# Expert stage of a routed MoE: row writes of further groups without a wait behind their issue, and the activation transpose inside the next expert's first product

## Chip, cores and metric

The kernel runs on one core of one Trainium2 chip. The metric is the device time of one execution in microseconds (us), as the median of several runs. An engine's names are as in the profile: PE is TensorE's matmul side and PEld its weight loads, DVE is VectorE, ACT is ScalarE, POOL is GpSimd, SP is SyncE, which here issues all plain DMAs.

## What is computed

One step of a decoder trunk with one layer, for 512 prompt tokens and 8 sample tokens of width 1024, all in float32. A mixer sub-layer (three parallel head groups behind one input projection, one output projection) comes first; the change doesn't touch it. The second sub-layer is the one that matters: a mixture of 32 experts, each a SwiGLU MLP with an inner width of 256.

```python
g_idx = argmax(h @ w_group)                                # one of 4 groups of experts
top_p, top_i = top_k(softmax(h @ w_router[g_idx]), 2)      # two of its 8 experts
combine = ...                                              # the weight of each expert for each token
gate = einsum('btd,edf->btef', h, w_gate)                  # w_gate, w_up: (32, 1024, 256)
up = einsum('btd,edf->btef', h, w_up)
act = silu(gate) * up * combine[..., None]
out = x + einsum('btef,efd->btd', act, w_down)             # w_down: (32, 256, 1024)
```

The kernel computes each expert only for the tokens routed to it.

## The kernel before

The expert stage stands at the end of the program, from about 546 to 850 us of the profiled execution. Ahead of it, VectorE ranks the tokens of each expert, and GpSimd scatters their numbers with ten indirect DMAs into `slot_table` (`tab` in the code). An expert has 64 slots (`CAP`); tokens past the 64th go to *further groups* of 64 slots. How many further groups an expert has is only known at run time: each engine loads the number from `more` and branches (`more_groups`), so each of PE, ACT, DVE and POOL runs its own `body` under the same conditions.

Experts are taken four to a round (`ROUND = 4`, u = 0 to 3), eight rounds, of which the first and the last are written out and the six between are a hardware loop. There are four weight slots, one for each u. SP loads an expert's `w_gate`, `w_up` and `w_down` (1 MB each) into slot u with three DMAs once VectorE has counted `expert_done` for the expert that used the slot before (`load_expert`); VectorE counts it after the expert's last copy, that of its further groups included. All these loads are in SP's queue in the order of the experts.

For each expert e, PE does the following:

- `up`: the first product, gate and up side by side, 16 steps in the code (8 chunks of the 1024 inner rows, for each half of the columns), 32 matmuls in the trace. It waits for the expert's weights and for `xT`, the gathered and transposed tokens of a pair of experts.
- a transpose of `gact`, the activations, into PSUM bank 2 (line 1952). Before it, ACT has taken the tanh of the gate (`tanh_gate`), and DVE has made `gact` of it in two instructions (`swiglu`, lines 1531 and 1533).
- `down`: the second product with `aT`, the transposed activations that ACT has copied out of PSUM (`act_T`), into bank 4 or 5. DVE copies the result to `ysb`, and POOL writes the rows to `expert_rows` (`yd` in the code) with an indirect DMA.

The products are staggered: within a round PE does `up` of experts 0 and 1, then the transpose and `down` of expert 0, `up` of expert 2, transpose and `down` of expert 1, `up` of expert 3, and so on; u = 3 has no `up` behind it. After the `up` of u = 0 and u = 2 PE also transposes the tokens of the next pair (`xg`, line 1949), which ACT copies to `xT` (`xT_out`). The rows `xg` are gathered by POOL with an indirect DMA.

A further group of expert e stands behind its `down`. POOL has gathered its rows to `xo[u % 2]`: for an expert's first group this happens two experts ahead, at the end of POOL's work for expert e - 2 (`first_further`, which calls `gather_more`: index to `otok` at line 1076, gather at line 1081). PE transposes the rows (lines 1962 and 1964), computes `up` into bank 3, transposes the activations (line 1969) and computes `down`, again into bank 3, with ACT and DVE between the steps, and DVE copies the result to `yo`. POOL writes `yo` out with one indirect DMA (line 1064, named `expert_rows<-yo,osid`). Three waits close this:

```python
# POOL, behind the write
pool.wait_ge(m_out, done * 16 + 16)
pool.sem_inc(m_saved, 1)
# DVE, ahead of the copy to yo
vec.wait_ge(m_saved, done + 1)
# PE, behind its last product of the group (bank 3 is free when yo is copied)
pe.wait_ge(m_vec, done * 3 + 3)
```

`done` counts the further groups that came before. On the inputs here there are four further groups, one each for the experts 17, 19, 23 and 24 (rounds 4, 4, 5 and 6).

Of the kernel before, what the change touches and what calls it, by code (L numbers as in the profile page):

```python
# [13 lines left out]
P = 128  # L26
D = 1024
KT = D // P
# [82 lines left out]
def build(nc, A, R):  # L111

    with ExitStack() as ctx:
# [246 lines left out]
        def pair(name):  # L360
# [33 lines left out]
        m_otok, m_osid, m_pe, m_act, m_vec, m_out, m_saved = (  # L394
            sem("more_" + n) for n in ("otok", "osid", "pe", "act", "vec", "out", "saved"))
# [61 lines left out]
        def _(sp):  # L457
# [94 lines left out]
            sp.wait_ge(tab_written, 2 * NT * 16)  # L552
# [31 lines left out]
        def _(act):  # L584
# [279 lines left out]
            def act_round(it, first, last):  # L864
                for u in range(ROUND):
                    e = ROUND * it + u
                    if u == 1 or (u == 3 and not last):
                        xT_out(2 * it + (u + 1) // 2, (u + 1) // 2 % 2)
                    if u < 3:
                        if u == 0:  # L870
                            tanh_gate(e, 0)
                        tanh_gate(e + 1, (u + 1) % 2)
                    act_T(e, u % 2)

                    def body(g, done, needed):
                        act.wait_ge(m_pe, done * 4 + 1)
                        copy(xTo[:, :, :].rearrange("p a b -> p (a b)"), ps[:, 3, :], ACT.Copy).then_inc(m_act, 1)
                        act.wait_ge(m_pe, done * 4 + 2)
                        copy(oth[:, :], ps[:, 3, 0:P], ACT.Tanh, scale=0.5).then_inc(m_act, 1)
                        act.wait_ge(m_pe, done * 4 + 3)  # L880
                        copy(oaT[:, :], ps[:, 3, 0:P], ACT.Copy).then_inc(m_act, 1)

                    more_groups(act, e, body)
# [26 lines left out]
        def _(pool):  # L910
# [97 lines left out]
            for i in range(NT):  # L1008
                pool.wait_ge(routed, 3 if i < SPLIT else 6)
                for n in range(2):  # L1010
                    nc.gpsimd.indirect_dma_start(out=tab, out_offset=bass.IndirectOffsetOnAxis(ap=where[:, n, i:i + 1], axis=0),  # L1011
                                                 in_=pid[:, n, i:i + 1], in_offset=None, bounds_check=MAXROWS * NE - 1,
                                                 oob_is_err=False).then_inc(tab_written, 16)
# [4 lines left out]
            pool.sem_inc(m_saved, 1)  # L1018
# [18 lines left out]
            def pool_round(it, first, last):  # L1037
                for u in range(ROUND):
# [16 lines left out]
                    def body(g, done, needed):  # L1055
                        nc.gpsimd.tensor_tensor(osid[:, :], osids[:, bass.ds(g * NE + column, 1)], zero[:, :], ALU.add).then_inc(
# [5 lines left out]
                        pool.wait_ge(m_vec, done * 3 + 3)  # L1062
# [4 lines left out]
                        pool.wait_ge(m_out, done * 16 + 16)  # L1067
                        pool.sem_inc(m_saved, 1)
# [27 lines left out]
            for u in range(ROUND):  # L1096
                pool.wait_ge(y_out[u], 16 * ROUNDS)
            pool.sem_inc(moe_done, 1)

        @block.vector  # L1100
        def _(vec):
# [423 lines left out]
            count_groups(vec, "vec")  # L1525
            vec.wait_ge(routed, 7)
# [9 lines left out]
            def vec_round(it, first, last):  # L1536
                for u in range(ROUND):
# [10 lines left out]
                    def body(g, done, needed):  # L1548
                        vec.wait_ge(m_act, done * 3 + 2)
                        stt(out=oact[:, :], in0=oth[:, :], scalar=1.0, in1=ps[:, 3, 0:P], op0=ALU.add, op1=ALU.mult).then_inc(m_vec, 1)  # L1550
                        vec.wait_ge(m_vec, done * 3 + 1)
                        stt(out=oact[:, :], in0=oact[:, :], scalar=0.5, in1=ps[:, 3, P:2 * P], op0=ALU.mult, op1=ALU.mult).then_inc(m_vec, 1)
                        vec.wait_ge(m_pe, done * 4 + 4)
                        vec.wait_ge(m_saved, done + 1)
                        nc.vector.tensor_copy(yo[:, :], ps[:, 3, :]).then_inc(m_vec, 1)
# [30 lines left out]
        def _(pe):  # L1586
# [329 lines left out]
            def halves(bank, left, right, steps, width):  # L1916
                for c in range(steps):
# [4 lines left out]
            def up(u, bank, left):  # L1922

                return halves(bank, left, lambda c, g: gu[u][:, :, c, g * P:(g + 1) * P], KT, 2 * P)

            def down(u, bank, a):
                return halves(bank, lambda c: a[:, c * CAP:(c + 1) * CAP], lambda c, g: wd[u][:, c, g * 512:(g + 1) * 512], 2, 512)

            def pe_up(it, u):
                e = ROUND * it + u  # L1930
                s = u // 2
                pe.wait_ge(weights_in[u], tiles_in[u] + 3 * 16 * (it + 1))
                pe.wait_ge(xT_ready, 2 * it + s + 1)
                up(u, u % 2, lambda c: xT[s][:, c, u % 2 * CAP:(u % 2 + 1) * CAP]).then_inc(up_done, 1)

            def pe_round(it, first, last):
                for u in range(ROUND):
                    e = ROUND * it + u
                    if u == 0:
                        pe_up(it, 0)  # L1940
                    if u < 3:
                        pe_up(it, u + 1)
# [8 lines left out]
                    pe.wait_ge(act_ready, e + 1)  # L1951
                    turn(ps[:, 2, 0:P], gact[u % 2][:, :], ident).then_inc(act_turned, 1)
# [3 lines left out]
                    def body(g, done, needed):  # L1956
                        pe.wait_ge(m_rows[u % 2], pe.snap(slot_groups[u % 2]) * 16 + 16)
                        pe.reg_add(slot_groups[u % 2], slot_groups[u % 2], 1)
                        for c in range(KT):
# [8 lines left out]
                        pe.wait_ge(m_vec, done * 3 + 2)  # L1968
# [3 lines left out]
                        pe.wait_ge(m_vec, done * 3 + 3)  # L1972
# [31 lines left out]
```

## Time and profile before

| | |
|---|---|
| time, median of 3 runs | 879.26 us (878.67 to 883.45) |
| profiled execution: span from its first to its last instruction | 876.5 us |
| what lies around the span, against the median | 2.8 us |
| PE, PEld busy | 680.9 us (78%), 493.8 us (56%) |
| DVE, ACT, POOL busy | 378.6, 201.0, 239.2 us |
| the mean DMA rate over the span, and in the expert stage at its fullest | 167 and 412 GB/s |
| the mean granted clock of PE | 0.895 of full |

The page of the profile gives no other time for the profiled execution than its span. Busy time is an average over stages with different limits: in the expert stage the loads of 96 MB of expert weights, PE's products and the short chains between the engines take turns in setting the pace, and a window or a chain of waits has to be read for each stretch.

### The profile page before, as it was taken

What the parts mean: (1) busy time and instruction counts of PE and PEld (TensorE: products, weight loads), DVE (VectorE), ACT (ScalarE), POOL (GpSimd) and SP (SyncE); (2) the same over time, 40 slices, a digit from 0 to 9 for tenths busy, and PEclk for the clock granted to TensorE, in tenths of its full rate; (3) what the DMA queues carried; (4) which work ended last, traced back from release to release, by engine and by line L of the source; (5) the groups of instructions that cost most, each with busy time, mean ns of one, the idle gap of its engine ahead of it and who ended that gap; (6) DMA issues with size and microseconds to landing.
All of it is one profiled execution on the core that took longest, in us unless ns stands there. A gap on an engine that the chain in (4) does not pass through costs nothing.

```text
span 876.5 us, 12140 instructions
## 1 busy us (share of the span) xinstructions
PE 680.9 (78%) x4468; PEld 493.8 (56%) x4469; DVE 378.6 (43%) x570; ACT 201.0 (23%) x401; POOL 239.2 (27%) x268
## 2 busy tenths in 40 slices
PE   2699978789889999978898840978889766978840
PEld 2699977679778889854344430544444433444410
DVE  3605999997347666546212453112112110111128
ACT  5113325634222341241001110101101110101103
POOL 1527479975230010110000024122122221321210
PEclk9989989889989999995889965899989997999985
DMA  9013322112071000035111541299999975895926
GB/s 278 26 49 98 97 73 71 51 49 54 6 247 65 1 1 1 1 118 198 32 48 49 191 168 28 69 413 408 410 414 405 410 310 213 313 386 222 404 75 246
DMA packets 73209, 146.70 MB, mean 167 GB/s; under 512 B 14568, under 2 KB 50604, under 8 KB 64831
## 3 DMA queue, kind: packets, MB, share of 16 engines
q1 hardware_dynamic: 67327, 137.38, 42.7%
q0 software_dynamic: 5824, 8.54, 2.8%
q8 instruction: 37, 0.61, 0.3%
q14 instruction: 21, 0.17, 0.1%
HBM read 139.65 MB, written 16.60 MB: 178 GB/s over the span
## 4 chain that ended last, share of the span: by engine, by line
PE 51%; DVE 25%; DMA 13%; issue 4%; ACT 4%; POOL 1%; SPq 1%; POOLq 0%; DVEq 0%; ACTq 0%
PE ps L1919 17%; DMA wd<-w_down 8%; PE ps L1709 8%; PE ps L1859 7%; PE ps L1636 7%; DVE yT L1179 6%; DVE acc L1189 4%; DMA xo<-h_rows,otok 1%; DVE XX L1355 1%; PE ps L1880 1%; DVE cv L1197 1%; DVE x L1568 1%; PE ps L1949 1%; PE ps L1619 1%; PE ps L1842 1%
## 5 line engine op out<-in xcount | busy, mean ns | idle before, releaser
L1919 PE MATMUL ps<-gu,xT 128*64 128x256 f32 x1024 | 128.3, 409 | 30.2 <-DMA wd<-w_down 15.0
L1636 PE MATMUL ps<-hhi,whi 128*128 128x256 f32 (+1 forms) x416 | 125.1, 301 | 18.7 <-POOL wlo L927 8.3
L1919 PEld LDWEIGHTS ps<-gu,xT 128*64 128x64 f32 x1024 | 80.6, 148 | 85.5 <-issue 35.4
L1636 PE MATMUL ps<-hhi,wlo 128*128 128x256 f32 (+1 forms) x416 | 122.9, 295 | 0.0
L1636 PE MATMUL ps<-hlo,whi 128*128 128x256 f32 (+1 forms) x416 | 122.7, 295 | 0.0
L1636 PEld LDWEIGHTS ps<-hhi,whi 128*128 128x128 f32 x416 | 84.4, 203 | 24.7 <-POOL wlo L927 15.9
L927 POOL TENSOR_TENSOR wlo<-wraw,whi 128x1024 fp32r<-128x1024 f32 x26 | 77.1, 2971 | 66.5 <-ACT whi L609 66.4
L1636 PEld LDWEIGHTS ps<-hhi,wlo 128*128 128x128 f32 x416 | 84.5, 203 | 0.0
L1636 PEld LDWEIGHTS ps<-hlo,whi 128*128 128x128 f32 x416 | 84.2, 202 | 0.0
L1531 DVE SCALAR_TENSOR_TENSOR gact<-gth,ps 128x128 f32<-128x128 f32 x32 | 9.2, 288 | 148.6 <-ACT gth L891 148.6
L1919 PE MATMUL ps<-wd,aT 128*64 128x512 f32 x256 | 62.0, 605 | 11.7 <-ACT aT L895 11.7
L1051 POOL DMA_INDIRECT expert_rows<-ysb,scur x32 | 32.4, 1014 | 141.0 <-DVE ysb L1546 137.4
L1859 PE MATMUL ps<-wout,yT 128*128 128x512 f32 x128 | 65.6, 671 | 0.0
L1179 DVE SCALAR_TENSOR_TENSOR yT<-ub,parab,yT 128x512 f32<-128x512 f32 x60 | 63.0, 1115 | 0.0
L891 ACT ACTIVATE gth<-ps 128x128 f32<-128x128 f32 x32 | 8.9, 278 | 187.6 <-PE ps L1919 180.2
L1546 DVE COPY ysb<-ps 128x512 f32<-128x512 f32 x32 | 22.1, 692 | 68.2 <-PE ps L1919 68.2
L1189 DVE SCALAR_TENSOR_TENSOR acc<-raw,parq,acc 128x544 f32<-128x544 f32 x36 | 44.9, 1246 | 6.1 <-ACT acc L704 5.2
L1859 PEld LDWEIGHTS ps<-wout,yT 128*128 128x128 f32 x128 | 26.7, 214 | 36.5 <-issue 36.4
L1011 POOL DMA_INDIRECT slot_table<-pid,where x10 | 9.9, 995 | 118.4 <-DVE where L1485 115.9
L1355 DVE TENSOR_TENSOR XX<-XX,ps 128x1024 f32<-128x1024 f32 (+1 forms) x24 | 27.0, 1130 | 26.2 <-PE ps L1709 26.2
L1919 PEld LDWEIGHTS ps<-wd,aT 128*64 128x64 f32 x256 | 15.5, 136 | 36.8 <-ACT aT L895 18.6
L1406 DVE TENSOR_TENSOR x<-x,ps 128x1024 f32<-128x1024 f32 x4 | 4.9, 1222 | 63.5 <-PE ps L1859 63.5
(360 smaller groups left out, 1062.8 us busy)
## 6 DMA issues: line engine op xcount, KB each, us to landing
gu<-w_gate SPq DMA_DIRECT2D x32, 1024.0 KB
gu<-w_up SPq DMA_DIRECT2D x32, 1024.0 KB
wd<-w_down SPq DMA_DIRECT2D x32, 1024.0 KB
wraw<-w_in SPq DMA_DIRECT2D x26, 512.0 KB
wout<-w_out SPq DMA_DIRECT2D x1, 4096.0 KB, 16.5
yk<-expert_rows SPq DMA_DIRECT2D x8, 512.0 KB, 6.4
x<-x_prompt SPq DMA_DIRECT2D x4, 512.0 KB, 5.7
s<-state_delta SPq DMA_DIRECT2D x4, 512.0 KB, 6.1
```

What stands on the lines that cost most here:

```text
L927: nc.gpsimd.tensor_tensor(wlo[s][:, :, :], wraw[s][:, :, :], whi[s][:, :, :], ALU.subtract).then_inc(w_lo, 1)
L1011: nc.gpsimd.indirect_dma_start(out=tab, out_offset=bass.IndirectOffsetOnAxis(ap=where[:, n, i:i + 1], axis=0), in_=pid[:, n, i:i + 1], in_ ...
L1051: nc.gpsimd.indirect_dma_start(out=yd, out_offset=bass.IndirectOffsetOnAxis(ap=scur[u][:, 0:1], axis=0), in_=ysb[u][:, :], in_offset=None, ...
L1179: ins = stt(out=y, in0=tap, scalar=parab[:, t, j:j + 1], in1=y, op0=ALU.mult, op1=ALU.add)
L1189: ins = stt(out=a[:, :], in0=r[:, j:j + CV], scalar=parq[:, QKV[m], j:j + 1], in1=a[:, :], op0=ALU.mult, op1=ALU.add)
L1355: tt(xx, xx, new, ALU.subtract).then_inc(X_ready, 1)
L1531: stt(out=gact[s][:, :], in0=gth[s][:, :], scalar=1.0, in1=ps[:, s, 0:P], op0=ALU.add, op1=ALU.mult).then_inc(act_half, 1)
L1546: nc.vector.tensor_copy(ysb[u][:, :], ps[:, 4 + u % 2, :]).then_inc(y_ready, 1)
L1636: last = mm(ps[:, 2 * (n % 2) + half, 0:hi - lo], weights[:, c, :], h[:, c, lo:hi], start=c == 0 and j == 0, stop=c == KT - 1 and j == len ...
L1709: last = mm(ps[:, bank, i * P:(i + 1) * P], left(i), right(i), start=True, stop=True)
L1859: last = mm(ps[:, 2 * (i % 2) + half, :], yT[:, k, tokens(ORDER[i])], wout[:, k, half * 512:(half + 1) * 512], start=k == 0, stop=k == KT - 1)
L1919: last = mm(ps[g * CAP:(g + 1) * CAP, bank, 0:width], left(c), right(c, g), start=c == 0, stop=c == steps - 1)
```

## The change

Four things are edited.

1. POOL no longer waits behind a further group's write. It waits for the previous group's write at the start of the next group's `body`, before it overwrites the index `osid`. `m_saved` is gone: DVE waits for `m_out` itself before it overwrites `yo`. So that the formulas hold for the first group, the last of the ten writes of `slot_table` counts in `m_out`, and a wait for `m_out` at the end of the stage is added.
2. PE no longer waits behind a further group. It waits at the start of the next group for the last group's copy to `yo`; DVE's count `m_vec` begins at 1.
3. PE's `up` of the next expert is cut in two halves of four chunks, with the transpose of this expert's activations between them.
4. ACT copies the transposed activations ahead of the next expert's tanh, and not behind it.

```diff
-            sp.wait_ge(tab_written, 2 * NT * 16)
+            sp.wait_ge(tab_written, (2 * NT - 1) * 16)
+            sp.wait_ge(m_out, 16)
...
-                    if u < 3:
-                        if u == 0:
-                            tanh_gate(e, 0)
-                        tanh_gate(e + 1, (u + 1) % 2)
-                    act_T(e, u % 2)
+                    if u == 0:
+                        tanh_gate(e, 0)
+                    act_T(e, u % 2)
+                    if u < 3:
+                        tanh_gate(e + 1, (u + 1) % 2)
...
+                    written = m_out if (i, n) == (NT - 1, 1) else tab_written
...
-            pool.sem_inc(m_saved, 1)
...
                     def body(g, done, needed):
+                        pool.wait_ge(m_out, done * 16 + 16)
...
-                        pool.wait_ge(m_vec, done * 3 + 3)
+                        pool.wait_ge(m_vec, done * 3 + 4)
...
-                        pool.wait_ge(m_out, done * 16 + 16)
-                        pool.sem_inc(m_saved, 1)
...
+            pool.wait_ge(m_out, pool.snap(groups_done[pool]) * 16 + 16)
             pool.sem_inc(moe_done, 1)
...
             count_groups(vec, "vec")
+            vec.sem_inc(m_vec, 1)
...
-                        vec.wait_ge(m_vec, done * 3 + 1)
+                        vec.wait_ge(m_vec, done * 3 + 2)
...
-                        vec.wait_ge(m_saved, done + 1)
+                        vec.wait_ge(m_out, done * 16 + 16)
...
-            def pe_up(it, u):
-                e = ROUND * it + u
-                s = u // 2
+            def pe_up_begin(it, u):
                 pe.wait_ge(weights_in[u], tiles_in[u] + 3 * 16 * (it + 1))
-                pe.wait_ge(xT_ready, 2 * it + s + 1)
-                up(u, u % 2, lambda c: xT[s][:, c, u % 2 * CAP:(u % 2 + 1) * CAP]).then_inc(up_done, 1)
+                pe.wait_ge(xT_ready, 2 * it + u // 2 + 1)
+                up(u, u % 2, lambda c: xT[u // 2][:, c, u % 2 * CAP:(u % 2 + 1) * CAP], range(KT // 2))
+
+            def pe_up_end(u):
+                up(u, u % 2, lambda c: xT[u // 2][:, c, u % 2 * CAP:(u % 2 + 1) * CAP], range(KT // 2, KT)).then_inc(up_done, 1)
+
+            def turn_act(e, u):
+                pe.wait_ge(act_ready, e + 1)
+                turn(ps[:, 2, 0:P], gact[u % 2][:, :], ident).then_inc(act_turned, 1)
...
                     if u == 0:
-                        pe_up(it, 0)
+                        pe_up_begin(it, 0)
+                        pe_up_end(0)
                     if u < 3:
-                        pe_up(it, u + 1)
+                        pe_up_begin(it, u + 1)
+                    turn_act(e, u)
+                    if u < 3:
+                        pe_up_end(u + 1)
...
-                    pe.wait_ge(act_ready, e + 1)
-                    turn(ps[:, 2, 0:P], gact[u % 2][:, :], ident).then_inc(act_turned, 1)
                     pe.wait_ge(aT_ready, e + 1)
                     down(u, 4 + u % 2, aT[u % 2]).then_inc(down_done, 1)
...
                         pe.reg_add(slot_groups[u % 2], slot_groups[u % 2], 1)
+                        pe.wait_ge(m_vec, done * 3 + 1)
...
-                        pe.wait_ge(m_vec, done * 3 + 2)
+                        pe.wait_ge(m_vec, done * 3 + 3)
...
-                        pe.wait_ge(m_vec, done * 3 + 3)
```

## Rows read from the trace of the kernel before

**Rows 1.** The page, part 4: shares of the chain that ended last, by line.

```profile
PE ps L1919 17%; DMA wd<-w_down 8%; PE ps L1709 8%; PE ps L1859 7%; PE ps L1636 7%; DVE yT L1179 6%; DVE acc L1189 4%; DMA xo<-h_rows,otok 1%; DVE XX L1355 1%; PE ps L1880 1%; DVE cv L1197 1%; DVE x L1568 1%; PE ps L1949 1%; PE ps L1619 1%; PE ps L1842 1%
```

**Rows 2.** Busy time by window: engines, granted clock, DMA share, GB/s.

```profile
600.00:650.00 50.00, 40.65 (x278) 21.02 (x276) 8.23 (x20) 6.38 (x15) 12.09 (x20) 0.97 1.02 412
705.00:710.00 5.00, 3.02 (x17) 0.85 (x13) 1.03 (x3) 0.56 (x2) 0.00 (x0) 1.00 0.51 206
795.00:800.00 5.00, 3.21 (x19) 1.31 (x21) 0.69 (x1) 1.30 (x2) 0.77 (x1) 1.00 0.15 29
```

**Rows 3.** The chain that ended last, in order of time: start, length, step.

```profile
711.10 6.81 DMA expert_rows<-yo,osid
...
720.22 6.94 DMA xo<-h_rows,otok
...
761.13 6.20 DMA xo<-h_rows,otok
...
817.01 18.59 DMA wd<-w_down
```

**Rows 4.** Waits, 540 to 876 us: total, times, longest.

```profile
PE ps L1919 <- ACT aT L895: 11.7, 32, 0.4
```

**Rows 5.** Timeline of round 5, ordinary experts: start, length, instruction, idle before.

```profile
744.11 0.28 ACT L891 ACTIVATE gth<-ps 128x128 f32<-128x128 f32 x1 [7.51 <-PE ps L1919]
...
744.75 0.29 DVE L1533 SCALAR_TENSOR_TENSOR gact<-gact,ps 128x128 f32<-128x128 f32 x1
...
750.64 3.31 PEld L1919 LDWEIGHTS ps<-gu,xT 128*64 128x64 f32 x32 [0.56 <-ACT xT L887]
...
756.81 3.62 PE L1919 MATMUL ps<-gu,xT 128*64 128x256 f32 x32
756.81 3.17 PEld L1919 LDWEIGHTS ps<-gu,xT 128*64 128x64 f32 x30 [0.29 <-issue]
```

**Rows 6.** Timeline, PE's first product behind each group, and a copy into yo.

```profile
709.55 0.69 DVE L1555 COPY yo<-ps 128x512 f32<-128x512 f32 x1 [2.82 <-PE ps L1919]
...
710.75 3.67 PE L1919 MATMUL ps<-gu,xT 128*64 128x256 f32 x32 [1.34 <-DVE yo L1555]
...
740.40 7.13 PE L1919 MATMUL ps<-gu,xT 128*64 128x256 f32 x64 [1.81 <-DVE yo L1555]
...
778.16 7.13 PE L1919 MATMUL ps<-gu,xT 128*64 128x256 f32 x64 [1.85 <-issue]
...
798.96 3.67 PE L1919 MATMUL ps<-gu,xT 128*64 128x256 f32 x32 [1.42 <-DVE yo L1555]
```

**Rows 7.** Timeline of GpSimd and PE from expert 17's row write to expert 23's group.

```profile
711.10 0.99 POOL L1064 DMA_INDIRECT expert_rows<-yo,osid  x1 [7.64 <-DVE yo L1555]
...
718.49 1.94 PE L1919 MATMUL ps<-wd,aT 128*64 128x512 f32 x8 [0.37 <-ACT aT L895]
...
719.17 0.18 POOL L1076 TENSOR_TENSOR otok<-otoks,zero 128x1 int32<-128x1 int32 x1 [7.08 <-issue]
...
727.29 0.66 PE L1962 MATMUL ps<-cst,xo 64*128 64x64 f32 x2 [6.87 <-DMA xo<-h_rows,otok]
...
760.07 0.18 POOL L1076 TENSOR_TENSOR otok<-otoks,zero 128x1 int32<-128x1 int32 x1 [0.50 <-issue]
...
767.46 0.40 PE L1962 MATMUL ps<-cst,xo 64*128 64x64 f32 x2 [1.03 <-DMA xo<-h_rows,otok]
```

**Rows 8.** Timeline: products behind idle times on PE, and expert 24's slot release.

```profile
616.17 8.81 PE L1919 MATMUL ps<-gu,xT 128*64 128x256 f32 x64 [3.32 <-issue]
...
686.02 5.06 PE L1919 MATMUL ps<-gu,xT 128*64 128x256 f32 x32 [4.27 <-DMA wd<-w_down]
...
798.16 0.33 SPq L516 DMA_DIRECT2D gu<-w_gate  x1
...
827.19 3.67 PE L1919 MATMUL ps<-gu,xT 128*64 128x256 f32 x32 [2.19 <-DMA wd<-w_down]
...
835.65 5.33 PE L1919 MATMUL ps<-gu,xT 128*64 128x256 f32 x32 [2.22 <-DMA wd<-w_down]
```

More of the change, by code:

```diff
@@ L393, in build @@
         m_rows = pair("more_rows")
-        m_otok, m_osid, m_pe, m_act, m_vec, m_out, m_saved = (
-            sem("more_" + n) for n in ("otok", "osid", "pe", "act", "vec", "out", "saved"))
+        m_otok, m_osid, m_pe, m_act, m_vec, m_out = (
+            sem("more_" + n) for n in ("otok", "osid", "pe", "act", "vec", "out"))
         fin_added, fin_ready = sem("fin_added"), sem("fin_ready")
@@ L1010, in _ @@
                 for n in range(2):
+                    written = m_out if (i, n) == (NT - 1, 1) else tab_written
                     nc.gpsimd.indirect_dma_start(out=tab, out_offset=bass.IndirectOffsetOnAxis(ap=where[:, n, i:i + 1], axis=0),
                                                  in_=pid[:, n, i:i + 1], in_offset=None, bounds_check=MAXROWS * NE - 1,
-                                                 oob_is_err=False).then_inc(tab_written, 16)
+                                                 oob_is_err=False).then_inc(written, 16)
             count_groups(pool, "pool")
@@ L1914, in _, with halves @@
             pe.wait_ge(routed, 7)
-            def halves(bank, left, right, steps, width):
-                for c in range(steps):
+            def halves(bank, left, right, steps, width, part):
+                for c in part:
                     for g in range(2):
@@ L1920, in halves, with up @@
                 return last
-            def up(u, bank, left):
-                return halves(bank, left, lambda c, g: gu[u][:, :, c, g * P:(g + 1) * P], KT, 2 * P)
+            def up(u, bank, left, part=range(KT)):
+                return halves(bank, left, lambda c, g: gu[u][:, :, c, g * P:(g + 1) * P], KT, 2 * P, part)
             def down(u, bank, a):
-                return halves(bank, lambda c: a[:, c * CAP:(c + 1) * CAP], lambda c, g: wd[u][:, c, g * 512:(g + 1) * 512], 2, 512)
-            def pe_up(it, u):
-                e = ROUND * it + u
-                s = u // 2
+                return halves(bank, lambda c: a[:, c * CAP:(c + 1) * CAP], lambda c, g: wd[u][:, c, g * 512:(g + 1) * 512], 2, 512,
+                              range(2))
+            def pe_up_begin(it, u):
                 pe.wait_ge(weights_in[u], tiles_in[u] + 3 * 16 * (it + 1))
-                pe.wait_ge(xT_ready, 2 * it + s + 1)
-                up(u, u % 2, lambda c: xT[s][:, c, u % 2 * CAP:(u % 2 + 1) * CAP]).then_inc(up_done, 1)
+                pe.wait_ge(xT_ready, 2 * it + u // 2 + 1)
[5 more added lines that the diff above has]
+                turn(ps[:, 2, 0:P], gact[u % 2][:, :], ident).then_inc(act_turned, 1)
             def pe_round(it, first, last):
```

## Prediction, made before the changed kernel had run

> **What bounds the kernel now.** I read the page first, for the shares of the chain that ended last: products of the experts and the loads of `w_down` stand high in it [rows 1]. Then the busy time by windows, because the expert stage (546 to 850 us) is not one regime. Up to about 707 us the DMA queues are full (412 GB/s, share above 1), so the weight loads set the pace; at 705 to 710 the share falls to 0.51, and at 795 to 800 it is 0.15: there the loads wait for a slot, and the slot for the experts' own chain [rows 2]. The chain of waits says it by name: up to the start of expert 17's product at 686.02 PE waits for `wd` again and again (4.27 us there [rows 8]); then come PE, one step for the write of `yo` and two for gathers into `xo`; from 817.01 a DMA step for `wd` again [rows 3]. So a saving before 686 is worth what it brings forward of the load queue, one between 686 and 798 counts in full, and one after 798.16 (expert 24 gives its slot free, the queue fills up again) only behind the last load's landing [rows 3, 8].
>
> Further groups run four times: experts 17, 19, 23 and 24. The products behind them on PE are the rows that begin at 710.75, 740.40, 778.16 and 798.96 [rows 6].
>
> **The transpose in the next product.** Now PE transposes the activations, waits while ACT copies them, and starts the down product: 0.37 us idle, 32 times, 11.7 in all [rows 4]. With the transpose in the middle of the next expert's first product, the copy runs under its second half. That holds for u = 0, 1, 2 of a round; u = 3 keeps its wait. The transpose itself (0.3 us) is only moved. That it waits for `act_ready` inside the product costs nothing: the half product in front of it is 1.8 us (half of 3.62, rows 5), the tanh and the two VectorE steps that it waits for take 0.93 together from the end of the product before (744.11 to 745.04 [rows 5]), and for u = 1, 2 they ran under the down product. On ACT the copy into `aT` comes off the path between tanh and the copy into `xT`; the third product of a round now waits for `xT`, its weight loads idle 0.56 us where the plain seam has 0.29, so I take 0.3 per round when there is no group at u = 0 [rows 5]. An ordinary round that PE paces so gives 3 x 0.37 + 0.3 = 1.4 us; at nothing if the xg gather or the weights are late instead.
>
> **PE no longer waits for `yo`.** After a group, PE is idle 1.34, 1.81, 1.85 and 1.42 us [rows 6]. Of the first, 0.83 is the copy (down's end at 710.75 - 1.34 = 709.41, the copy ends at 709.55 + 0.69 = 710.24) and 0.51 is PE's own sequencer behind the wait. Without the wait the sequencer does that work under the down product (1.94 us), as it does behind an ordinary expert, where no idle time shows at 756.81 [rows 5]. Bounds: 0.83 for each, or the whole of it. I take all but 0.2, as the ordinary seam is the nearest row: 1.14, 1.6, 1.65; the fourth lies behind the last slot release that matters.
>
> **GpSimd no longer waits for the row write.** Expert 17's write is issued at 711.10 and lands 6.81 later [rows 3]; only then does GpSimd load the index of expert 19's first group (719.17) and gather it, which lands for PE at 727.29, while PE had finished expert 19's down product at 718.49 + 1.94 = 720.43: 6.87 idle [rows 7]. The other three writes hide: behind expert 19 and 23 GpSimd next waits for PE's xg transposes, behind 24 it has 7 us in hand. In the new kernel the write's instruction (0.99) ends 0.86 + 0.99 after the copy (710.24 to 711.10, rows 6 and 7), the index follows 0.5 (an ordinary expert's seam [rows 7]) to 1.2 later (719.17 less the write's landing at 717.9), the gather is issued 1.05 after the index, and takes 6.2 to 6.94 [rows 3].
>
> **The sum, in the profile's own times.**
> - Expert 0 is done 0.37 earlier, so load 4, which opens the full queue, is too; expert 17's weights land at 685.65: 0.37.
> - Round 4: u = 0 and its xT wait 0.67, u = 1 0.37: the group of 17 starts 1.4 earlier.
> - Behind it 1.14 (2.55), expert 18 another 0.37: expert 19's down product ends at 720.43 - 2.9 = 717.5.
> - The `yo` copy ends at 708.85, the write starts at 709.7, ends at 710.7, index 711.5, gather 712.6, landing 719.1 (bounds 718.4 and 719.9). PE's start moves from 727.29 to 719.1: 8.2.
> - The clock: the group of 19 ran from 727.29 to 738.59 = 11.30 us at the low clock, behind 6.87 of standstill; the group of 23 ran from 767.46 to 776.31 = 8.85 behind an idle time of 1.03 [rows 6, 7]. With 1.6 idle now the second holds: 2.4, together 10.6.
> - Behind 19: 1.6 (12.2). Round 5: 0.67 + 0.37 (13.3); its u = 2 saves nothing, since PE waits for the gather of expert 23 already (1.03, rows 7), which hangs on expert 21's write. Behind 23: 1.65 (14.9). Expert 24, u = 0: 0.37 (15.3).
> - So the slot that the row at 798.16 fills is free 15.3 earlier. From there to the last landing the queue is full, as loads 30 and 31 land a load's time apart [rows 8]; later slots are free 15.3 to 17 earlier, so it stays full, and the last weights land 15.3 earlier (835.65 to 820.35).
> - The tail: expert 30's down product has no gap (0.37). PE reaches the third product of the last round earlier than its weights, by 4 us instead of 2.19, so that this one will run slowly; it ends just as the last weights land, and the last product then starts behind almost no idle time and takes 3.67 and not 5.33 [rows 8]. Of these 1.66 I take 1.2 (bounds: minus 0.5, if the slow product itself is late, and 1.66).
>
> Together 15.3 + 0.37 + 1.2 = 16.9 us: a span of 859.6 for 876.5. Around the span lie 2.8 us against the median of 879.26, which I leave, so 862.4.
>
> **Does the load queue take it back?** The last two loads land 8.46 us apart in the full queue (827.19, 835.65 [rows 8]). From 707 on eleven loads are left (21 to 31): 93 us, so never ready before 800, and I forecast 820.35. The queue is still idle before loads 21, 23, 24 and 28, some 20 us in all, as the slots dictate. Expert 23's load is the tightest: its slot is free when the copy behind expert 19's group ends, at about 728, so it is there by 738, and its product starts at 743.
>
> **The rule of the clock.** Rows first: products started at full rate behind idle times of 1.03, 1.34, 1.42, 1.81, 1.85 and 2.19 us, and at the low level (1.2 GHz) behind 2.22, 3.32, 4.27 and 6.87 [rows 6, 7, 8]. The Trainium skill, TensorE: Matmul & The Clock Gate, section "HAM oscillation — how this bites in real kernels", says that a wait for a transfer between products throttles PE, so that the next products start cold. Taken so broadly it would keep 11.30 for expert 19's group and the sum would be 14.5, the time 864.8. The trace agrees for the long waits and not for the short ones.
>
> **Rivals.**
> 1. The clock stays low at expert 19's group, or the gather comes late (719.9) and brings it down. For: 2.19 and 2.22 lie on either side, and 1.6 may be 2.4. Against: five shorter waits cost nothing. Time: 862.4 + 2.4 + 0.8 = 865.6.
> 2. The post-group waits hide only the copy (0.83 each) and the transpose inside the product gives half of its gap (seven of 0.37 count): 862.4 + 1.9 + 1.3 + 1.2 (tail) = 866.8. For: these rows have no precedent in the trace.
> 3. The gather is not earlier, since it queues behind the write and load 21 in the DMA engines: PE's standstill of 6.87 stays, so of 8.2 only 2.9 are won, and the 2.4 of the clock are lost: 862.4 + 5.3 + 2.4 = 870.1. Against: the gather at 761.13 was issued right behind expert 21's row write (its index at 760.07 comes 0.5 after that instruction), while loads ran, and took 6.20 [rows 3, 7].
> 4. Slower than before: stalls of issue. At 616.17 PE stood 3.32 us at the head of a round with no wait named [rows 8]; the head of the round before shows the like. The Trainium skill, Runtime: NRT & Kernel Launch, section "Instruction fetch mechanics", says that a taken branch out of the fetched window stalls the engine for a fetch; no row proves that this is one. The code around each branch moves now. From six such stalls between 686 and the end (of some 15 branches over group code) 6 x 3.3 = 19.8 outweigh the gain: 882. Against: no such stall stood in that stretch before, and PE's sequencer gets more lead, not less.
>
> **Chances.** Forecast 0.58, rival 1 0.17, rival 2 0.13, rival 3 0.08, rival 4 0.02, and 0.02 for no change (within 0.5%, 4.4 us, about what a measurement can tell). Faster by over 0.5%: 0.95; same 0.03; slower 0.02. The range: below, whole post-group gaps (0.6), expert 17's product at full clock (1.4, it took 5.06, rows 8), a fast gather (0.7), the tail (0.5) give 859.2, and jitter takes it to 858.5; above it reaches over rivals 1 and 2 to 868.5.
>
> **What would show it.** Right: the chain has no step for the `yo` write; index for `xo` within 1.5 us of the write's end; PE's idle time at expert 19's group under 2.5 us; `PE <- ACT aT` 8 times and not 32; the rows behind the groups without a wait for `yo`; PE's last `wd` wait ending near 820. Wrong: the queue empty before 707, a new wait for `xg`, or a low clock at expert 19's group.

## The result, and the profile after

The changed kernel takes 870.66 us (median of 16 runs, 865.99 to 874.01) against 878.64 for the kernel before (16 runs): ratio 0.9909, 95% interval 0.9889 to 0.9929. So it is 0.9% faster, where 862.4 us and a range of 858.5 to 868.5 had been forecast. The profiled execution took 871.0 us with a span of 869.2.

What had been done away with is gone. In the chain that ended last there is no step for the write of `yo` any more; two gathers into `xo` stand there, and the long steps for `wd`, the last of which begins at 808.45 where before it was 817.01 [rows 3]. But there are two steps called "issue" in the middle of the stage, of 6.52 and 3.37 us, and `q14`, one of the two queues of the kind "instruction" on the page and "the fetch queue" from here on, has 46 packets. The chain of waits of the changed kernel (start, length, step), and its page (parts 3 and 4):

```profile
672.37 18.23 DMA wd<-w_down
...
718.63 6.42 DMA xo<-h_rows,otok
...
738.63 6.52 issue
745.75 3.37 issue
756.70 6.56 DMA xo<-h_rows,otok
...
808.45 20.26 DMA wd<-w_down
```
```profile
q14 instruction: 46, 0.38, 0.1%
...
PE 48%; DVE 25%; DMA 15%; issue 5%; ACT 3%; POOL 1%; SPq 1%; POOLq 1%; DVEq 0%; ACTq 0%
```

The same queue on the page of the kernel before:

```profile
q14 instruction: 21, 0.17, 0.1%
```

The timeline of PE in the changed kernel (start, length, instruction, idle time before it and what ended it):

```profile
690.64 3.68 PE L1910 MATMUL ps<-gu,xT 128*64 128x256 f32 x16 [4.17 <-DMA wd<-w_down]
...
694.66 2.60 PE L1910 MATMUL ps<-gu,xT 128*64 128x256 f32 x16
...
714.65 1.90 PE L1910 MATMUL ps<-gu,xT 128*64 128x256 f32 x16
...
725.18 0.43 PE L1962 MATMUL ps<-cst,xo 64*128 64x64 f32 x2 [1.04 <-DMA xo<-h_rows,otok]
...
726.73 5.35 PE L1910 MATMUL ps<-gu,xTo 128*64 128x256 f32 x32 [0.69 <-ACT xTo L866]
...
735.56 5.35 PE L1910 MATMUL ps<-gu,xT 128*64 128x256 f32 x48
...
757.04 1.09 PE L1950 MATMUL ps<-cst,xg 128*128 128x128 f32 x8 [1.66 <-DMA xg<-h_rows,gcur]
...
763.39 0.43 PE L1962 MATMUL ps<-cst,xo 64*128 64x64 f32 x2 [0.83 <-DMA xo<-h_rows,otok]
...
820.15 1.95 PE L1910 MATMUL ps<-gu,xT 128*64 128x256 f32 x16 [1.67 <-DMA wd<-w_down]
...
828.75 3.34 PE L1910 MATMUL ps<-gu,xT 128*64 128x256 f32 x16 [2.80 <-DMA wd<-w_down]
```

Behind the groups PE now goes on without a wait: 714.65 and 735.56 carry no idle time, where before 1.34 and 1.81 stood [rows 6]. Expert 19's group waits 1.04 for its gather and not 6.87 [rows 7]. But its product at 726.73 takes 5.35 us for 32 matmuls, which take 3.67 at full rate. Two things are new: expert 17's first product starts at 690.64, 4.6 later than before (686.02 [rows 8]), and at 757.04 PE waits 1.66 for the rows of `xg`, a wait that the kernel before did not have. The timeline of GpSimd in the changed kernel, same columns:

```profile
615.91 1.00 POOL L1041 DMA_INDIRECT expert_rows<-ysb,scur  x1 [0.89 <-DVE ysb L1537]
623.88 0.18 POOL L1020 TENSOR_TENSOR gcur<-gidx,zero 128x1 int32<-128x1 int32 x1 [6.97 <-issue]
629.21 1.05 POOL L1023 DMA_INDIRECT xg<-h_rows,gcur  x1 [5.15 <-issue]
...
693.35 0.19 POOL L1020 TENSOR_TENSOR gcur<-gidx,zero 128x1 int32<-128x1 int32 x1 [5.35 <-issue]
698.78 1.05 POOL L1023 DMA_INDIRECT xg<-h_rows,gcur  x1 [5.25 <-issue]
...
716.52 0.99 POOL L1055 DMA_INDIRECT expert_rows<-yo,osid  x1 [7.67 <-DVE yo L1546]
717.54 0.20 POOL L1065 TENSOR_TENSOR otok<-otoks,zero 128x1 int32<-128x1 int32 x1
718.63 0.97 POOL L1070 DMA_INDIRECT xo<-h_rows,otok  x1 [0.88 <-POOL otok L1065]
...
745.42 0.18 POOL L1020 TENSOR_TENSOR gcur<-gidx,zero 128x1 int32<-128x1 int32 x1 [7.00 <-issue]
749.34 1.05 POOL L1023 DMA_INDIRECT xg<-h_rows,gcur  x1 [3.74 <-issue]
```

From the row write (716.52) to the index (717.54) and the gather (718.63) the order is as the forecast had it. At the head of a looped round, though, the index `gcur` comes 6.97, 5.35 or 7.00 us after the instruction before it, with no wait named, and its gather another 5.15, 5.25 or 3.74 later, where the index and the gather of other experts need 0.9. The view of waits sums it up for 540 to 870 us (total, times, longest):

```profile
POOL gcur L1020 <- issue: 37.5, 11, 7.1
...
POOL xg L1023 <- issue: 25.6, 6, 5.2
...
PE ps L1910 <- ACT aT L884: 2.9, 8, 0.4
```

In the kernel before the first of these was 5.4 us in all, the longest 1.2, and the second did not exist. The third is the small edit at work: 2.9 us in 8 waits for 11.7 in 32 [rows 4].

**Where the time went, by segments.** Both kernels (and the runs below) are cut at the same events: PE's first transposes of `xg` (546.94 before, 547.21 after), expert 17's first product, PE's start of the groups of experts 19 and 23, the slot release of expert 24 (798.16 before [rows 8], 791.92 after), PE's last wait for `wd`, the end. Durations are differences of such starts; the forecast column is worked out from the steps of the prediction (685.65, 719.1, 782.86, 820.35, 859.6).

```
us                                  before forecast  changed  12 more  +244 on   PE's wait
                                                              (below)  before    alone
start of the stage                  546.94   546.94   547.21   548.69   550.43   549.33
to expert 17's first product        139.08   138.71   143.43   138.86   144.31   139.41
to the group of expert 19            41.27    33.45    34.54    32.87    42.41    42.30
to the group of expert 23            40.17    35.13    38.21    35.42    41.33    40.18
to expert 24's slot release          30.70    28.63    28.53    28.54    30.70    30.34
to the last wait's end for wd        37.49    37.49    36.83    36.54    37.44    38.41
to the end                           40.85    39.25    40.45    40.18    39.18    39.13
```

The changed kernel misses its forecast by 9.6 us, and 8.9 of them stand in three lines: 4.7 up to expert 17's product, 1.1 up to the group of 19, 3.1 up to the group of 23 (in this last line stand the slow product, 1.7, and the wait for `xg`, 1.66). Another 1.2 is the tail, 0.3 is the later start, and 0.8 come back in the two lines between. The start of the stage varies by up to 4 us from one profiled execution to another, which is why the segments and not the spans are compared. Each column is one profiled execution.

### The profile page after: what moved, and what is told of

The parts are those of the page before. It is cut to its first block, busy times and chain, and to the rows that moved or that the text cites. A ratio compares the mean times of both kernels' runs of the same rounds, so it can differ in the third digit from the quotient of the medians.

```text
span 869.2 us, 12127 instructions
## 1 busy us (share of the span) xinstructions
PE 686.3 (79%) x4468; PEld 491.4 (57%) x4469; DVE 378.4 (44%) x570; ACT 201.1 (23%) x401; POOL 237.0 (27%) x268
## 4 chain that ended last, share of the span: by engine, by line
PE 48%; DVE 25%; DMA 15%; issue 5%; ACT 3%; POOL 1%; SPq 1%; POOLq 1%; DVEq 0%; ACTq 0%
PE ps L1910 13%; DMA wd<-w_down 11%; PE ps L1700 8%; PE ps L1850 7%; PE ps L1627 7%; DVE yT L1169 6%; DVE acc L1179 5%; DMA xo<-h_rows,otok 1%; DVE XX L1345 1%; PE ps L1871 1%; DVE x L1559 1%; PE ps L1610 1%; PE ps L1833 1%; PE ps L1650 1%; PE ps L1814 1%
## 5 line engine op out<-in xcount | busy, mean ns | idle before, releaser
L1910 PE MATMUL ps<-gu,xT 128*64 128x256 f32 x1024 | 135.7, 416 | 30.9 <-DMA wd<-w_down 25.5
L1910 PEld LDWEIGHTS ps<-gu,xT 128*64 128x64 f32 x1024 | 76.8, 148 | 87.8 <-DMA wd<-w_down 30.1
L1179 DVE SCALAR_TENSOR_TENSOR acc<-raw,parq,acc 128x544 f32<-128x544 f32 x36 | 49.9, 1386 | 6.1 <-ACT acc L693 5.3
L884 ACT ACTIVATE aT<-ps 128x128 f32<-128x128 f32 x32 | 8.9, 277 | 111.2 <-PE ps L1931 111.2
```

The costliest lines, as they stand in the source:

```text
L1179: ins = stt(out=a[:, :], in0=r[:, j:j + CV], scalar=parq[:, QKV[m], j:j + 1], in1=a[:, :], op0=ALU.mult, op1=ALU.add)
L1910: last = mm(ps[g * CAP:(g + 1) * CAP, bank, 0:width], left(c), right(c, g), start=c == 0, stop=c == steps - 1)
```

## Experiments

The edits have names: **GpSimd's wait** (the wait for `m_out` moved from behind the row write to the next group's beginning, with `m_saved` gone and the last table write counted on `m_out`), **PE's wait** (the wait for the copy into `yo` moved from the group's end to the next group's beginning, counts of `m_vec` one higher), and **the transpose** (PE's and ACT's order). Four kernels, with the kernel before, ran on one chip (before: 879.33), four on a second (879.07) and two on a third (879.12).

### The changed kernel once more

> The changed kernel once more, beside the others of this set. Theory F (GpSimd stands still at the head of every hardware-loop round, 5 to 7 us before the index instruction of the xg gather and 5 us behind it, which the kernel before didn't): the same two gaps again, in each of the five looped rounds and in no other place. Theory C (longer waits for weights put PE on the low clock, products and slot releases come later, the full load queue runs short): expert 17's product again starts later than the 686.0 of the kernel before. Theory N (the 4.6 us lost ahead of expert 17 are chance): its start varies by some us from run to run. All: ratio to before near 0.991.

871.5 us (868.65 to 876.28), ratio 0.9922 (0.9894 to 0.9949). The stalls of GpSimd, the wait for `xg` (1.76) and the late expert 17 (142.70 us after the stage's start) came again, so they are no accident of one execution. One thing did not come again: the product of 19's group ran at full rate, behind 0.94 us of idle time, with the group reached 178.40 us after the stage's start (177.97 in the execution above).

```profile
726.33 3.67 PE L1910 MATMUL ps<-gu,xTo 128*64 128x256 f32 x32 [0.69 <-ACT xTo L866]
```

### Twelve instructions more on GpSimd

Nothing of the change is taken back; GpSimd's program only gets twelve instructions near its beginning, on a semaphore that nobody waits for.

```diff
             link = linker(pool, s_pool)
+            for _ in range(12):
+                pool.sem_inc(pool_passed, 1)
```

> The changed kernel with 12 added increments of an unused semaphore at GpSimd's start, which shift its round loop to the place in the instruction stream that it has in the kernel before. Theory F: the gaps of 5 to 7 us are gone, the xg gather of round 5 is no longer late (1.66 us of PE idle), the time is 1.5 to 5 us under that of the changed kernel. Theory C and N: gaps gone or not, the time stays within 1 us of the changed kernel.

863.59 us (860.3 to 868.53), ratio 0.9834 (0.98 to 0.9867): 7.9 us faster than the changed kernel beside it (871.5), by twelve instructions that do nothing. That is more than the 1.5 to 5 us that had been expected. The page has 21 packets in the fetch queue and no step of 6 us of issue in the chain; GpSimd's timeline has a gap of 1.32 and one of 0.89 where 6.97 and 5.15 stood:

```profile
q14 instruction: 21, 0.17, 0.1%
```
```profile
619.72 0.18 POOL L1022 TENSOR_TENSOR gcur<-gidx,zero 128x1 int32<-128x1 int32 x1 [1.32 <-issue]
620.79 1.05 POOL L1025 DMA_INDIRECT xg<-h_rows,gcur  x1 [0.89 <-POOL gcur L1022]
```

And PE in the same run:

```profile
687.55 3.41 PE L1912 MATMUL ps<-gu,xT 128*64 128x256 f32 x16 [4.38 <-DMA wd<-w_down]
...
720.42 0.43 PE L1964 MATMUL ps<-cst,xo 64*128 64x64 f32 x2 [0.61 <-DMA xo<-h_rows,otok]
...
721.98 3.67 PE L1912 MATMUL ps<-gu,xTo 128*64 128x256 f32 x32 [0.69 <-ACT xTo L866]
...
755.84 0.43 PE L1964 MATMUL ps<-cst,xo 64*128 64x64 f32 x2 [1.43 <-DMA xo<-h_rows,otok]
...
820.92 3.29 PE L1912 MATMUL ps<-gu,xT 128*64 128x256 f32 x16 [2.77 <-DMA wd<-w_down]
```

Expert 17's first product is back at 138.86 us behind the stage's start, the wait for `xg` is gone, and the group of 19 is computed at full rate (3.67). Expert 24's slot is released 784.38 - 548.69 = 235.69 us behind the start, where the forecast had 782.86 - 546.94 = 235.92.

### The kernel before, moved

The place of GpSimd's round loop in its instruction stream, counted in the built programs: it begins at instruction 485 in the kernel before, at 473 in the changed one (the edits make the code ahead of the loop shorter by 12, and the loop itself by 8, 287 for 295), and at 485 with the twelve. If that decides, the kernel before must show the stalls as well once its loop is put elsewhere, though nothing of the change is in it.

```diff
+            for _ in range(244):
+                pool.sem_inc(pool_passed, 1)
             pool.wait_ge(slots_in, 16)
```

> The kernel before, with 244 increments of an unused semaphore where GpSimd idles (from 405 to 515 us), so that its round loop begins at the same place modulo 256 instructions as in the changed kernel. Theory F (the place of GpSimd's loop in the instruction stream decides whether its code is fetched again in each round): gaps of 5 to 7 us at the heads of rounds, 46 packets or so on the instruction queue instead of 21, expert 17's product 4 to 6 us later measured from the first xg transpose, and 3 to 7 us slower than before. Rival (the gain of the shifted kernel comes from something in the changed code): same time as before.

886.32 us, ratio 1.0084 (1.0061 to 1.0106): the kernel before became slower by 7.3 us, a little more than the 3 to 7 expected. Its loop begins at 729 = 473 + 256. The increments stand where GpSimd waits anyway, ahead of the stage. Its page, GpSimd's timeline and PE's:

```profile
q14 instruction: 48, 0.39, 0.1%
```
```profile
625.78 0.18 POOL L1032 TENSOR_TENSOR gcur<-gidx,zero 128x1 int32<-128x1 int32 x1 [7.00 <-issue]
631.09 1.05 POOL L1035 DMA_INDIRECT xg<-h_rows,gcur  x1 [5.13 <-issue]
```
```profile
694.74 5.83 PE L1921 MATMUL ps<-gu,xT 128*64 128x256 f32 x32 [4.66 <-DMA wd<-w_down]
...
772.22 1.09 PE L1951 MATMUL ps<-cst,xg 128*128 128x128 f32 x8 [1.69 <-DMA xg<-h_rows,gcur]
```

Both effects are there, in a kernel without the change: expert 17's product 144.31 us behind the stage's start for 139.08, and a wait for `xg` of 1.69. Against the thought that so many more instructions cost by themselves stand the next two.

### A shift by 128, and one by 6

Both on the changed kernel: 128 increments at the idle place of the last run, and 6 at the beginning.

> The changed kernel with 128 added increments on GpSimd, in its idle time ahead of the slot table. GpSimd's round loop is 287 instructions long. If its code is fetched in pieces of 128 instructions, the loop touches as many pieces as in the changed kernel: gaps and 46 packets, ratio to before 0.991. If in pieces of 256, it touches one less: no gaps, 21 packets, ratio 0.983.

> The changed kernel with 6 added increments at GpSimd's start, halfway to the 12 that took the gaps away. Theory F: it is one or the other, gaps and 0.991 or no gaps and 0.983, and nothing between, since only the piece in which the loop's first or last instruction lies can count. Rival (each added instruction delays GpSimd a little, and that orders the DMAs better): between the two, near 0.987.

With 128 more (loop at 601) 871.82 us, ratio 0.9924 (0.9896 to 0.9952), as the changed kernel without them; with 6 more (loop at 479) 864.76 us, ratio 0.9836 (0.9814 to 0.9858), as with twelve. The page and a row of GpSimd, first of the kernel with 128 more:

```profile
q14 instruction: 48, 0.39, 0.1%
```
```profile
621.23 0.18 POOL L1022 TENSOR_TENSOR gcur<-gidx,zero 128x1 int32<-128x1 int32 x1 [7.17 <-issue]
```

and of the kernel with 6 more, whose fetch queue has 21 packets:

```profile
618.58 0.18 POOL L1022 TENSOR_TENSOR gcur<-gidx,zero 128x1 int32<-128x1 int32 x1 [1.27 <-issue]
```

So it is the place that decides and not the number of instructions: loops that begin at 473, 601 and 729 stall, those at 479 and 485 do not. The three that stall leave the same remainder by 128 (89), and a packet of the fetch queue is on average 0.38 MB / 46 = 8.2 KB.

That the stalls are fetches can be read from the times of the queue's packets in the traces. In each of the five traces that stall, 23 to 25 packets of 8 KB run between 624 and 829 us; in each of the seven that do not, none does. And they lie inside the gaps: in the changed kernel at 618.9, 621.0 and 621.7 in the gap of 6.97 us, and at 626.9 in the one of 5.15 behind it, with at least one packet in every long gap at the heads of the later rounds too. Most of these packets run for 0.3 us, so the greater part of a gap is waiting around them. The Trainium skill, Runtime: NRT & Kernel Launch, section "Instruction fetch mechanics", says that a taken branch whose target is outside of a window of two pages stalls the engine for a fetch. The trace agrees with the stall: 11 to 12 us a round in two pieces, and 25 packets more. It does not agree with the page's block of 16 KiB or 256 instructions for this queue: a shift by 128 instructions brings the same pattern back, and the packets are half a block long. Which blocks of the loop are fetched again, and why six instructions are enough to end it, stays open.

### The parts of the change

First the two waits without the transpose, and the transpose alone, both without shift:

> Edits 1 and 2 alone (no wait behind the row write, none on PE behind the group), the transpose stands ahead of the down product as before. By my prediction's terms: 1.14 + 5.3 + 2.4 + 1.6 + 1.65 = 12 us faster than before at the slot release of expert 24. Theory C: expert 17 starts at 686 as before, and this kernel is as fast as the changed one or faster (ratio 0.986 to 0.99). Theory F: GpSimd's gaps are here as well, and the ratio is 0.990 to 0.995.

> Edits 3 and 4 alone, all waits as before. By my prediction's terms: 0.37 + 1.04 + 0.37 + 1.04 + 0.37 + 0.37 = 3.6 us faster than before. Theory C: nothing or slower (ratio 0.998 to 1.005), with expert 17 starting 2 to 5 us late. Theory F: GpSimd's loop stands where it stood before, no gaps there, and the ratio is 0.995 to 0.997.

The waits alone: 875.34 us, ratio 0.995 (0.9929 to 0.9971), with 46 packets and the stalls (the longest 7.34 us), 4.0 faster where 12 had been worked out without stalls; these are the edits that shorten GpSimd's code. The transpose alone: 876.15 us, 0.996 (0.9942 to 0.9978), no stalls of the fetch, 3.2 us faster where the steps of the prediction give 3.6. It touches no line of GpSimd's. (Its GpSimd has two gaps called "issue" of 7.47 and 7.15 us too, but behind row writes whose landing it waits for, and without a packet of the fetch queue in them: the name alone does not tell a fetch.)

Then the waits with twelve increments at the beginning (as above), and GpSimd's wait alone with them, and PE's wait alone, where GpSimd's code keeps its place:

```diff
                     def body(g, done, needed):
+                        pe.wait_ge(m_vec, done * 3 + 1)
...
-                        pe.wait_ge(m_vec, done * 3 + 3)
```

> Edits 1 and 2 with the 12 added increments. Theory F: no gaps, 21 packets; the clean worth of the two edits, by my prediction's terms 1.14 + 5.3 + 2.4 + 1.6 + 1.65 = 12.1 us (ratio 0.986). Rival: as without the increments (ratio 0.995).

> Edit 1 alone (GpSimd doesn't wait behind the row write; PE still waits behind the group) with the 12 added increments. Theory F: no gaps, 21 packets, 5.3 + 2.4 = 7.7 us faster than before (ratio 0.991). If the low clock at expert 19's group stays: 5.3 us (0.994).

> Edit 2 alone (PE doesn't wait behind the group; GpSimd's wait and code stay, its loop stands where it stood before). 1.14 + 1.6 + 1.65 = 4.4 us faster than before if all counts (ratio 0.995); of it the 1.14 ahead of expert 19 may go into the longer wait for the gather: 3.3 us (0.996).

Both waits: 867.27 us, ratio 0.9868 (0.9839 to 0.9897), 11.8 faster. GpSimd's wait alone: 871.41, ratio 0.9911 (0.9892 to 0.9931), 7.7 faster, as worked out. PE's wait alone: 878.44, ratio 0.9984 (0.9964 to 1.0004), 0.6 faster and so not told from no change; there 3.3 to 4.4 had been expected, a miss. The rows of PE in this last kernel:

```profile
688.74 6.65 PE L1920 MATMUL ps<-gu,xT 128*64 128x256 f32 x32 [4.11 <-DMA wd<-w_down]
...
731.04 0.68 PE L1964 MATMUL ps<-cst,xo 64*128 64x64 f32 x2 [7.93 <-DMA xo<-h_rows,otok]
...
763.64 1.09 PE L1950 MATMUL ps<-cst,xg 128*128 128x128 f32 x8 [0.39 <-DMA xg<-h_rows,gcur]
...
771.22 0.43 PE L1964 MATMUL ps<-cst,xo 64*128 64x64 f32 x2 [1.50 <-DMA xo<-h_rows,otok]
```

Its GpSimd, behind the row write of expert 19's group:

```profile
753.73 0.18 POOL L1030 TENSOR_TENSOR gcur<-gidx,zero 128x1 int32<-128x1 int32 x1 [7.61 <-issue]
```

PE leaves the group of 17 earlier and stands the longer for the gather of 19's rows, 7.93 us for 6.87 [rows 7], as GpSimd sends that gather only once the row write has landed. Behind the group of 19 the same: GpSimd issues the next index only behind the write's landing (a gap of 7.61 us), so `xg` is late by 0.39 and the rows of 23 by 1.50. PE's wait is worth 871.41 - 867.27 = 4.1 us beside GpSimd's wait, and 0.6 without it: the one makes the other count. The times alone would not prove it (their intervals are 1.7 to 2.6 us wide to either side); the longer waits in these rows say where the gain went. About 1.0 of the miss may be another thing, the first product at 688.74, which took 6.65 us for 5.06 before [rows 8] and made the row write of 17 later by as much (26.6 us behind that product's start for 25.1).

## Why the forecast was wrong, step by step

**The step that failed.** It is the first of the sum: "expert 17's weights land at 685.65". In the changed kernel PE could start on them only at 690.64. In its repetition they landed 142.65 us behind the stage's start, where 138.71 had been forecast. Behind it stands what the prediction put into its fourth rival, priced at 0.02: that code which moves can stall an engine for its fetch. The mechanism was the right one, but I looked for it on PE, where stalls of 3.3 us already stood, and gave it a price by PE's branches. It struck GpSimd, whose loop head was quiet before (gaps of at most 1.2 and 0.9); the sum had no term for GpSimd's code outside of the edited lines: that was put at nothing without a reason. Taking the stalls away again, with all edits in place, brought 7.9 us, nearly the whole miss. "No such stall stood in that stretch before" was the argument against, and it holds only as long as the code stays where it is.

**How a stall on GpSimd reaches PE.** Two ways: the first goes together with the stalls in every trace but is not followed link by link, the second is read directly.

First, in the stretch with full queues. GpSimd is not late for PE there, but the loads are. An expert's weights are three matrices, each split over 16 DMA engines, so a load has 48 landing records. The numbers are how long the last record comes behind the fourth last, in us, for the loads 4 to 31 of four runs: if one engine is behind, its three pieces are the last three. (In the kernel before, 49 of 1344 records are missing from the trace; each load there is taken from those it has.)

```
changed        1.5 1.3 1.0 1.5 1.5 1.4 1.8 3.1 3.8 3.1 4.9 6.5 6.0 5.4 5.9 7.5 6.1 1.0 0.2 1.1 0.8 2.1 1.9 2.6 0.2 0.7 0.7 1.4 mean 2.68
before         0.8 1.9 1.2 1.6 1.0 1.7 0.8 1.3 1.1 0.7 0.9 0.8 0.7 1.6 0.7 1.2 0.8 0.2 0.2 0.1 0.5 3.4 2.7 0.8 0.1 0.6 0.9 1.5 mean 1.07
12 more        1.0 1.0 0.9 1.2 1.5 1.2 0.8 1.0 1.4 0.7 0.8 0.8 0.6 1.2 0.6 0.8 0.6 0.6 0.4 0.1 0.1 0.3 0.8 0.8 0.2 0.6 0.7 1.4 mean 0.79
before, +244   1.1 1.9 1.0 1.3 1.1 1.6 2.1 2.9 4.1 3.4 5.2 6.2 5.8 5.9 5.7 7.2 5.7 0.1 0.6 0.0 0.9 1.9 2.0 1.4 0.2 0.4 0.8 1.5 mean 2.57
```

The other eight traces fall on the same two sides: means of 2.37, 2.45 and 2.67 in the three more executions that stall, 0.76 to 0.99 in the five that do not. In load 15 of the changed kernel the last record comes 3.0 us behind the second last, 6.2 behind the third last and 6.5 behind the fourth last: that looks like one engine with its three pieces, up to 7.5 us behind the others, and a load counts as landed only with its last piece. The whole shows in where load 17 lands: 142.7 to 145.3 us behind the stage's start in the five traces that stall, 138.5 to 139.5 in the seven that do not. The window view of the changed kernel shows the loss; the columns are the window and its length, busy us of PE, PEld, DVE, ACT, POOL, then granted clock, DMA share and GB/s.

```profile
600.00:650.00 50.00, 41.46 (x254) 20.42 (x252) 8.04 (x19) 6.13 (x14) 10.87 (x18) 0.90 1.01 405
650.00:690.00 40.00, 29.61 (x206) 14.96 (x202) 5.63 (x14) 4.55 (x11) 9.40 (x15) 0.95 1.00 400
700.00:705.00 5.00, 4.94 (x41) 2.75 (x41) 1.01 (x3) 0.55 (x2) 1.27 (x3) 1.00 0.71 230
```

and of the kernel before:

```profile
650.00:690.00 40.00, 31.74 (x204) 16.90 (x206) 5.30 (x13) 4.24 (x10) 9.69 (x16) 0.87 1.01 409
700.00:705.00 5.00, 4.31 (x41) 2.71 (x39) 0.69 (x1) 0.60 (x1) 1.24 (x2) 1.00 1.01 420
```

405 and 400 GB/s where the kernel before had 412 [rows 2] and, from 650 to 690, 409; and at 700 to 705 the queue is not full (share 0.71, before 1.01), which fits 15 engines that have run out while one still works. That the slow engine is the one which carries the fetches, and that it is the waiting fetches which hold it up, is argued from this pattern and not shown: no record names the engine of a fetch. What is shown is that the place of the loop switches both on and off together.

Second, behind 707, where the loads wait for slots. The gather of `xg` for experts 24 and 25 is issued at 749.34, behind stalls of 7.00 and 3.74; PE waits for it 1.66 at 757.04. It is the "new wait for `xg`" that the prediction named as a sign against itself, and it stands in all five traces that stall (1.39 to 1.76 us). Two products of the changed kernel also ran in part at the lower of the two levels of the clock: expert 17's, behind 4.17, took 3.68 for its first 16 matmuls and 2.60 for the second 16 (1.95 at the full rate; granted clock 0.50 and 0.74), and the one of 19's group 5.35 (granted clock 0.68). In the repetition neither did.

**The other steps.**
- The transpose in the product: right. 8 waits of 0.37, 2.9 in all; alone it brought 3.2 of the 3.6 forecast.
- PE's wait for `yo`: right beside GpSimd's wait, and even the whole of each gap was saved (no idle time at 714.65, 735.56, 772.10 and 791.12), where all but 0.2 was counted. But it was costed as if it stood for itself, and alone it brought 0.6, not told from nothing.
- GpSimd's wait: right. The index came 1.02 us behind the write's issue, the gather 1.09 later, and took 6.42; forecast were 1.8, 1.1 and 6.5. Alone it brought 7.7.
- The clock at the group of 19: right without the stalls (3.67 behind 0.61 us of idle time, 720.42 and 721.98 in the run with twelve more), wrong in the profiled execution of the changed kernel (5.35 behind 1.04), and right again in its repetition (3.67 behind 0.94) and with 128 more (3.67 behind 1.12). So in that execution the 2.4 of the step were got only in part: 725.18 to 735.56 is 10.38 us, 11.30 before and 8.72 with twelve more. An idle time of 1.03 before had been followed by full rate, one of 1.04 now was not, and in the same trace a product behind 3.21 us of waiting ran at full rate (1.95 for 16 matmuls at 673.48, granted clock 1.00): the length of the last idle time alone does not tell the level, and the prediction's line between 2.19 and 2.22 does not hold. Nor does the rule of the Trainium skill, TensorE: Matmul & The Clock Gate, section "HAM oscillation — how this bites in real kernels", that a wait for a transfer leaves the next products cold, when it is read as broadly as the prediction read it: it fits the products behind 1.04 and 4.17, and not those behind 0.94, 1.12 and 3.21.
- The rivals: the time of the third, 870.1, is near the one measured by luck and not by its mechanism; the gather did not queue up (6.42 us, PE idle for 1.04 and not for 6.87). The first came true in part, with the slow product of 19's group in one execution. The second did not: the waits behind the groups went whole.
- The full queue behind 798: right. The last wait for `wd` ended 36.83 us behind the slot release (37.49 before).
- The tail: mis-sized. Of 0.37 + 1.2 forecast 0.4 came (40.85 to 40.45). The third product of the last round was not slow, as its wait was 1.67 and not 4, and the last one was: it waited 2.80 and took 3.34 for its first 16 matmuls. The bound that was named for it, minus 0.5, was nearer.

The gain that was forecast came only without the stalls. With them out of the way the sum holds: the kernel with twelve increments measured 15.7 us below the one before (863.59 for 879.33), where 16.9 had been worked out, and 0.9 of the missing 1.2 is the tail (39.25 forecast, 40.18 measured).

## What to carry to other kernels

An edit that makes an engine's program longer or shorter ahead of a hardware loop moves that loop, and this alone cost 8 us of 870 here, as much as the whole measured gain. Look at the packets of the instruction queues on the page before and after each edit, and then for gaps called "issue" at the heads of looped rounds; if they changed, put a few idle instructions ahead of the loop and time again, before a reason is sought in the edit itself. And where two engines wait in turn for one event, taking the wait from one of them is worth little until the other has lost its own: cost such edits together and not as a sum.

## What was not expected of the hardware

- At the head of each looped round GpSimd stands still twice for a fetch. While the DMA queues are full it takes 5 to 7 us each time (6.97 and 5.15; the 7.00 before 745.42 also, with a DMA share of 1.00), and it is hardly shorter when they are not: 3.74 before 749.34 (share 0.52 from 745 to 750) and 5.14 before 787.02 (share 0.38 from 782 to 787).
- Six instructions decide: a loop that begins at 473 stalls, at 479 not (871.5 and 864.76 us).
- Twenty-five fetch packets more, 0.2 MB of 147, go with loads whose last pieces come up to 7.5 us behind the others.
- The best of all kernels here is the changed one with twelve increments, 863.59 us, 0.9834 of the kernel before (0.98 to 0.9867).
